# First modulation vectors of a two-block transformer kernel: the last weight quarter by column halves, the second weight chunk loaded behind it, one quarter by VectorE alone, first conversions moved

## The reference, cut to what matters

```python
ada = silu(c) @ ada_w[l] + ada_b[l]                 # nine vectors of 1024 per layer
shift, scale, gate = first three of them            # for the first feed-forward layer
n = rms_norm(x, norm_g) * (1 + scale) + shift
x = x + gate * ((silu(n @ ffn_wg) * (n @ ffn_wu)) @ ffn_wd)      # then attention, further layers, the second block
```

## Time and profile before

| | us |
|---|---|
| median of 3 runs | 2181.8 |
| profiled execution, its own time | 2183.51 |
| its span | 2181.7 |
| TensorE busy | 2120.3 (97%) |
| VectorE busy | 1777.2 (81%) |
| ScalarE busy | 1175.9 (54%) |
| share of the chain that ended last: PE, DVE, DMA | 89%, 7%, 2% |

### The profile page before, as it was taken

The page is one execution under the profiler, slowest core; times in us unless marked ns, Lnnn a source line. Parts: engine busy times, 40 slices in busy tenths (PEclk is TensorE's granted clock), DMA queues, the critical chain, the costliest instruction groups (busy, mean ns, idle before and its releaser), DMA issues.

```text
span 2181.7 us, 33428 instructions
## 1 busy us (share of the span) xinstructions
PE 2120.3 (97%) x13811; PEld 1857.7 (85%) x13820; DVE 1777.2 (81%) x2350; ACT 1175.9 (54%) x1759; POOL 109.5 (5%) x157
## 2 busy tenths in 40 slices
PE   7999999999999999999999999999999999999997
PEld 4888888888888888898888989988888888778886
DVE  4888787788878878977888877898998998777764
ACT  3555556555455445565553544547646744575742
POOL 1000000000000000000000000000000000000000
PEclk9999999999999999999999999999999999999999
DMA  9889675478868877655888747738878877315662
GB/s 331 288 274 317 219 245 193 155 252 282 312 196 276 281 272 234 228 188 171 278 276 286 235 161 223 244 126 291 281 268 292 295 255 248 117 35 160 212 212 78
DMA packets 331024, 506.51 MB, mean 232 GB/s; under 512 B 12392, under 2 KB 239943, under 8 KB 330872
## 3 DMA queue, kind: packets, MB, share of 16 engines
q1 hardware_dynamic: 288647, 342.01, 47.7%
q0 software_dynamic: 41616, 160.44, 21.3%
q10 hardware_dynamic: 608, 1.92, 0.3%
HBM read 503.29 MB, written 1.05 MB: 231 GB/s over the span
## 4 chain that ended last, share of the span: by engine, by line
PE 89%; DVE 7%; DMA 2%; ACT 1%; issue 1%; POOL 0%; DVEq 0%; POOLq 0%
PE banks L635 38%; PE banks L639 19%; PE banks L629 7%; PE banks L631 6%; PE banks L630 6%; DMA plain_xs<-in_ada_w_dram 1%; PE banks L841 1%; PE banks L903 1%; PE banks L736 1%; PE banks L738 1%; PE banks L737 1%; DVE wlo L2056 1%; PE banks L1404 1%; DVE nraw L2334 1%; DMA stage<-in_ffn_wg_dram 1%
## 5 line engine op out<-in xcount | busy, mean ns | idle before, releaser
L2056 DVE TENSOR_TENSOR wlo<-stage,whi 128x1024 fp32r<-128x1024 f32 x644 | 758.3, 1219 | 124.4 <-ACT whi L1519 123.3
L1519 ACT CAST whi<-stage 128x1024 fp32r<-128x1024 f32 x644 | 643.8, 1052 | 336.5 <-PE banks L639 257.9
L635 PE MATMUL banks<-xs,whi 128*128 128x512 f32 x2176 | 688.1, 398 | 13.6 <-DVE xs L2338 9.5
L639 PEld LDWEIGHTS banks<-xs,wlo 128*128 128x128 f32 x2176 | 409.9, 188 | 97.0
L639 PE MATMUL banks<-xs,wlo 128*128 128x256 f32 x2176 | 428.6, 278 | 0.0
L629 PE MATMUL banks<-xs,whi 128*128 128x256 f32 x1216 | 351.1, 289 | 10.4 <-DVE xs L2338 5.6
L635 PEld LDWEIGHTS banks<-xs,whi 128*128 128x128 f32 x2176 | 332.2, 189 | 18.7 <-DVE xs L2338 7.6
L630 PE MATMUL banks<-xs,whi 128*128 128x256 f32 x1216 | 343.9, 283 | 0.0
L631 PE MATMUL banks<-xs,wlo 128*128 128x256 f32 x1216 | 343.9, 283 | 0.0
L635 PE MATMUL banks<-hidden_arena,whi 128*128 128x512 f32 x992 | 311.8, 395 | 0.0
L2081 DVE SCALAR_TENSOR_TENSOR arena<-modw,cact,arena 128x1024 f32<-128x1024 f32 x217 | 277.9, 1280 | 10.5 <-DMA modw<-in_w_mod_dram 6.7
(11 more groups left out here) (442 smaller groups left out, 2620.7 us busy)
## 6 DMA issues: line engine op xcount, KB each, us to landing
stage<-in_mlp_w_dram SPq DMA_DIRECT2D x96, 1024.0 KB, 5.4
modw<-in_w_mod_dram POOLq DMA_DIRECT2D x80, 1024.0 KB, 6.0
modw<-in_ada_w_dram POOLq DMA_DIRECT2D x66, 1024.0 KB, 5.5
stage<-in_ffn_wg_dram SPq DMA_DIRECT2D x44, 1024.0 KB, 5.5
stage<-in_ffn_wu_dram SPq DMA_DIRECT2D x44, 1024.0 KB, 7.4
stage<-in_ffn_wd_dram SPq DMA_DIRECT2D x44, 1024.0 KB, 7.4
stage<-in_ev_w_in_dram SPq DMA_DIRECT2D x24, 1024.0 KB, 5.9
stage<-in_w_in_dram SPq DMA_DIRECT2D x18, 1024.0 KB, 5.4
```

Of the source, the lines that this page charges most:

```text
L635: return mm(out, whi[:, s, w:w + P], pair.rearrange("p a t -> p (a t)"), start=first_mm, stop=False, skip_group_check=True)
L639: return mm(out[:, 0:T], wlo[:, s, w:w + P], pair[:, 0, :], start=False, stop=last_mm, skip_group_check=True)
L1519: nc.scalar.copy(halves(whi[:, s, :], n, h, True), halves(stage[:, s, :], n, h)).then_inc(hi_done, 1)
L2056: last = v.tensor_tensor(halves(wlo[:, s, :], n, h, True), halves(stage[:, s, :], n, h), halves(whi[:, s, :], n, h, True).bitcast(F32), AL ...
```

## The change

Transfer 7 goes into `modw` place 0 (where transfer 0 was) instead of `xs`; POOL waits before it until TensorE and VectorE have used transfer 0. SP loads chunk 1 only when transfer 7 has landed. Quarter 1 of the scale vector is done by VectorE alone (both rows), so TensorE's accumulator wait counts five products. The last quarter of the shift vector is done in column halves on both engines, and the partition sums follow each half. `conv(0)` on ScalarE moves in front of the normalised activations, `conv(1)` is split around `shifted_hi`; on VectorE the two halves of `conv(0)` stand between the products of vector 1. The first product of vector 1 stands ahead of vector 0's end. Two `keep_warm` groups of four go, the last one shrinks from ten to four.

```diff
-                      6: stage[:, 2, :], 7: words2(plain_xs)}
-        quarter = lambda c: start_room.get(c, modw[:, c % 2, :])
+                      6: stage[:, 2, :]}
+        quarter = lambda c: start_room.get(c, modw[:, 1 if c == 1 else 0, :])
...
-                        sp.wait_ge(start_landed[3], 16)
+                        sp.wait_ge(start_landed[7], 16)
...
+                if c == 7:
+                    pool.wait_ge(pe_out.sem, pe_out.at("row00"))
+                    pool.wait_ge(first_step[0], 1)
...
-            def row_rest(i):
+            def row_rest(i, h):
 
-                pe.wait_ge(first_step[i], 4)
-                for h in range(2):
-                    mm(first_rows[i][:, h, :], ones, first_acc[i][:, h * 512:h * 512 + 512],
-                       start=False, stop=True, skip_group_check=True).then_inc(pe_out.sem, pe_out.next((f"rows{i}", h)))
+                pe.wait_ge(first_step[i], 5 if i == 0 else 4 + h)
+                mm(first_rows[i][:, h, :], ones, first_acc[i][:, h * 512:h * 512 + 512],
+                   start=False, stop=True, skip_group_check=True).then_inc(pe_out.sem, pe_out.next((f"rows{i}", h)))
...
-            row_step(0, 1)
-            keep_warm(R[:, 3, :], 4)
             row_step(0, 2)
-            keep_warm(R[:, 3, :], 4)
             row_step(0, 3)
-            row_rest(0)
+            for h in range(2):
+                row_rest(0, h)
...
-            for q in range(1, 4):
+            for q in range(1, 3):
                 row_step(1, q)
-            row_rest(1)
+            for h in range(2):
+                row_step(1, 3, (h,))
+                row_rest(1, h)
             pe.wait_ge(act_out.sem, act_out.at(("F0", "n")))
-            keep_warm(Y[:, 3, :], 10)
+            keep_warm(Y[:, 3, :], 4)
...
+                        if k == 4:
+                            conv(1, (0,))
...
+            conv(0)
             act.wait_ge(dve_out.sem, dve_out.at("first_scale"))
...
-            conv(0)
-            conv(1)
             act.dma_start(base[:, FIRST_W:BASE_W], A["const"][:, FIRST_W:BASE_W]).then_inc(base_landed, 16)
...
             shifted_hi("F0", lambda k: mc(("ada", 0, 0), k))
+            conv(1, (1,))
             ffn("F0")
...
-            for q in range(3):
-                first_steps(0, q)
+            first_steps(0, 0)
+            first_steps(0, 1)
+            first_steps(0, 1, second=True, steps=2)
+            first_steps(0, 2, steps=3)
...
-            first_steps(0, 3)
+            first_steps(0, 3, steps=4)
+            first_steps(1, 0)
             own("pcol")
...
-            for q in range(4):
-                first_steps(1, q)
-            conv(0)
+            first_steps(1, 1)
+            conv(0, (0,))
+            first_steps(1, 2)
+            conv(0, (1,))
+            for h in range(2):
+                first_steps(1, 3, at=512 * h, width=512, steps=3 + h)
             done(first_vector(1, 0), ("first_shift", 0))
```

More of the change, by code:

```diff
@@ L918, in turn_rows, with row_step @@
                 last.then_inc(pe_out.sem, pe_out.next(("turned", s)))
-            def row_step(i, q):
+            def row_step(i, q, halves=(0, 1)):
                 pe.wait_ge(start_landed[4 * i + q], 16)
                 t = 2 * q + 1
-                for h in range(2):
-                    mm(first_rows[i][:, h, :], cact[:, 0, t:t + 1].to_broadcast([P, P]), quarter(4 * i + q)[:, 1024 + h * 512:1536 + h * 512],
-                       start=q == 0, stop=False, skip_group_check=True)
-            def row_rest(i):
-                pe.wait_ge(first_step[i], 4)
-                for h in range(2):
-                    mm(first_rows[i][:, h, :], ones, first_acc[i][:, h * 512:h * 512 + 512],
-                       start=False, stop=True, skip_group_check=True).then_inc(pe_out.sem, pe_out.next((f"rows{i}", h)))
+                for h in halves:
+                    last = mm(first_rows[i][:, h, :], cact[:, 0, t:t + 1].to_broadcast([P, P]),
+                              quarter(4 * i + q)[:, 1024 + h * 512:1536 + h * 512], start=q == 0, stop=False, skip_group_check=True)
+                return last
+            def row_rest(i, h):
+                pe.wait_ge(first_step[i], 5 if i == 0 else 4 + h)
+                mm(first_rows[i][:, h, :], ones, first_acc[i][:, h * 512:h * 512 + 512],
+                   start=False, stop=True, skip_group_check=True).then_inc(pe_out.sem, pe_out.next((f"rows{i}", h)))
             keep_warm(Y[:, 3, :], 12)
             pe.wait_ge(act_out.sem, act_out.at("cact"))
-            row_step(0, 0)
+            row_step(0, 0).then_inc(pe_out.sem, pe_out.next("row00"))
             keep_warm(R[:, 3, :], 4)
@@ L1508, in done, with conv @@
                 ins.then_inc(act_out.sem, act_out.next(key))
-            def conv(n):
+            def conv(n, part=(0, 1)):
                 if n >= NCH:
@@ L1517, in conv @@
                     act.wait_ge(chunk_used, n - RING + 1)
-                for h in range(2):
+                for h in part:
                     nc.scalar.copy(halves(whi[:, s, :], n, h, True), halves(stage[:, s, :], n, h)).then_inc(hi_done, 1)
@@ L2299, in rms, with first_steps @@
                     take_mod(Y[:, 2:4, :])
-            def first_steps(i, q):
+            def first_steps(i, q, second=False, at=0, width=1024, steps=None):
                 dve.wait_ge(start_landed[4 * i + q], 16)
-                w, cc = quarter(4 * i + q)[:, 0:1024], cact[:, 0, 2 * q:2 * q + 1]
+                w = quarter(4 * i + q)[:, 1024 * second + at:1024 * second + at + width]
+                cc = cact[:, 0, 2 * q + second:2 * q + second + 1]
+                acc = first_acc[i][:, at:at + width]
                 if q == 0:
-                    v.tensor_scalar(first_acc[i], w, cc, None, ALU.mult).then_inc(first_step[i], 1)
+                    v.tensor_scalar(acc, w, cc, None, ALU.mult).then_inc(first_step[i], 1)
                 else:
-                    dve.wait_ge(first_step[i], q)
-                    v.scalar_tensor_tensor(out=first_acc[i], in0=w, scalar=cc, in1=first_acc[i], op0=ALU.mult, op1=ALU.add) \
+                    dve.wait_ge(first_step[i], q if steps is None else steps)
+                    v.scalar_tensor_tensor(out=acc, in0=w, scalar=cc, in1=acc, op0=ALU.mult, op1=ALU.add) \
                         .then_inc(first_step[i], 1)
@@ L2315, in first_vector @@
                 vec = first_vectors[i]
-                own_step(i)
+                dve.wait_ge(first_step[i], 5 if i == 0 else 4 + h)
                 at = slice(h * 512, h * 512 + 512)
```

2 lines of the change are left out of this document (removed).

## The result

The changed kernel takes 2186.63 us (median of 15 runs, 2184.47 to 2190.86) against 2182.32 us (15 runs) before: ratio 1.0023, 95% interval [1.0016, 1.003]. The forecast was 2180.0, the range ended at 2185.4, and slower had a chance of 0.09. Its profiled execution took 2189.12 us, with a span of 2187.3 and a mean granted clock of 0.993 (before: 2183.51, 2181.7, 0.996).

A forecast was written before the change was run, and what follows sets the result against it. Bound: TensorE's chain of waits, with transfer 7 and chunk 2 ahead of it. Late start +2.4, chunk 2's wait -4.1 and clock -2.7, chunk 3's wait +2.6 gave -1.8: from 2181.8 to 2180.0 us, range 2176.0 to 2185.4.

The forecast's parts named there:

- Vector 0: Quarter 1's second row moves from TensorE to VectorE: vector 0 comes some 2 us sooner, worth nothing.
- Chunk 0 in front: ScalarE's cast waits for chunk 0 landing at 32.5 us; VectorE's first half product with transfer 7 ends at 37.7.
- The sums: TensorE's half-group sums of the shift vector: at full clock the second half is ready at 40.6 us, against 37.9 before.
- The clock: TensorE's clock halves around the sums: second half ready at 42.8 us, between bounds of 40.6 and 43.5.
- Chunk 2: Issued at 42.8 us, without the constants' load beside it, it lands in 8.2 us instead of 15.4, at 51.0.
- TensorE again: First layer starts 2.4 to 3.2 us late, no wait at chunk 2; chunk 3 ready at 63.9, a 2.6 us wait.
- The sum: Adds late start +2.4, chunk 2's wait -4.1 and clock -2.7, chunk 3's wait +2.6: -1.8 us.
- new wait at chunk 3 +2.6: TensorE, done with chunk 2 at 61.3 us, waits 2.6 us until chunk 3 is ready at 63.9.
- -1.8: Forecast change in when TensorE starts chunk 3, and so in the end: 63.9 instead of 65.7 us.
- No clock loss: Rival, chance 0.17: the clock stays up at the sums, chunk 3 ready at 61.7 us, -4.0, 2177.8 us.
- Shared from the start: Rival, chance 0.16: POOL's transfers run beside chunk 2 at once, it lands 14 to 15.4 us after issue; +3.5 to +4.9.
- Chunk 0 sooner: Rival, chance 0.09: chunk 0 lands 4 us or more sooner, chunk 3 ready at 58.6, -7.1, 2174.7 us.

The follow-up runs named there:

- e3: The kernel before with only ScalarE's load of the constants issued ahead of chunk 1's casts: 2178.76 us, ratio 0.9984 to before.
- w4: The changed kernel with 16 small products put ahead of TensorE's wait at chunk 3: 2183.99 us, ratio 1.0005 to before.
- w5: The changed kernel with 12 small products ahead of the shift vector's sums and 16 ahead of the wait at chunk 3: 2182.61 us, ratio 1.0 to before.
- the second timing: The changed kernel, unchanged, timed again against the kernel before on another chip: 2185.23 us, ratio 1.0017.
- e1: The changed kernel with chunk 0's cast put back where it was, on ScalarE and on VectorE: 2179.72 us, ratio 0.999 to before.

## Why the prediction was wrong

*Vector 0, Chunk 0 in front, The sums, The clock: right in mechanism.* ScalarE's cast at 32.28 (32.5 forecast), VectorE's first half of `wlo` at 33.35 (33.5), the first sum at 37.63 (37.8), a wait of 0.6 for transfer 7. A half product takes 0.8, above both bounds (0.64, 0.75). Vector 0 came 1.0 us sooner and not 2, which is worth nothing either way. In the first profile the clock fell at 38.9, behind the first sum and not ahead of it as forecast (in the other three at 35.8 to 36.9, ahead of it), and chunk 2 was issued at 41.95 (42.8). So the layer's third tile began at 44.53, 1.2 us later than before instead of 2.4.

*Chunk 2: mechanism right, size off.* It landed after 5.6 us instead of 8.2, with 833 packets in the first 4.07 us (836 forecast) and none of POOL's; e3 shows the cause. Nothing hung on the 2.6 us, since TensorE came later anyway.

*TensorE again: the number right, by two errors.* Chunk 3 landed at 58.7, not 60.5. But "two casts and two subtractions" was too little: TensorE waits for L2121, with four other operations of VectorE (L2441 to L2444) ahead of it behind `wlo`, 1.8 us more. Both cancel to 63.9: luck.

*The sum: this step failed.* It ended with "new wait at chunk 3 +2.6" and set nothing for the clock behind that wait, though the same sum took 2.7 us for the clock behind a wait of 4.11. The wait was 3.77 us, since TensorE was through with chunk 2 at 60.1 instead of 61.3, by the smaller late start, and chunk 3 took 2.7 us longer: -1.8 became +1.0. w4 and w5, which hold the clock up there, put the mark 2.2 and 1.8 us ahead. This step is 2.7 of the 6.1 us between the forecast's -1.8 and the first timing's +4.3 (of 4.4 us to the second's +2.6); the other 3.4 (1.7) lie behind the start by the marks, and their cause stays open. At 2.6 us, between the 1.08 that cost nothing and the 4.11 that did, the clock was an unknown that wanted both bounds; I took one without saying so. The Trainium skill, "TensorE: Matmul & The Clock Gate", section "Why this matters for your kernels", which I had named for the wait ahead of the sums, says that idle gaps between matmul bursts lower the clock; the trace agrees for this wait as well (0.50 behind 3.77 us).

*The rivals.* No clock loss: no. Shared from the start: no, POOL gave chunk 2 its head start; slower came by a way that I had not listed. Chunk 0 sooner: by 0.2 us in the first profile and up to 1.4 in the others, not 4.

*What no step had.* One execution of before stood for all; one of its other two profiles has late half clock, and the starts lie 2.1 us apart. That the second timing's 2185.2 lies inside the range, where the first's 2186.6 does not, says nothing for the sum, whose sign was wrong in both.

## What to carry to other kernels

When a wait is forecast to move and not to go, charge the new place all that the old place paid, the clock behind it included. An early conversion put ahead of work that is ready turns its transfer's landing into everybody's wait (e1: 5.5 to 6.9 us); look first which small load runs beside the late one, because moving it can be a gain by itself (e3: 3.5 us from one line). Single profiles of such a kernel differ by 2 us at 100 us and by 7 at the end, so a forecast of under 0.2% is read from timed runs.

## What the hardware did that I had not expected

A wait of 1.94 us near 1,950 us is followed by 3.4 us at half clock in some executions and by none in others, with the same program and the same wait. A load of 0.72 MB on ScalarE's queue beside a 1 MB chunk sets the chunk back by 10 us (15.4 against 5.4 in e3), where its own bytes would take 1.8 us by an estimate from the 0.39 MB per us of the earlier trace rows. In the first 4.07 us the chunk moved 308 packets instead of the 833 of the changed kernel, and what was left went beside POOL's transfers; how that adds up to 10 us, no run here shows.
